# Transposes moved between halves of products, scores of two row halves interleaved, and head outputs turned by pairs, in two transformer blocks on one core

## The chip, the cores and the metric

One core of a Trainium2 chip runs the kernel in one launch. The metric is the device time in microseconds, the median of the runs. TensorE's work is named by its MATMUL rows; a transpose is a matmul against the identity and is a MATMUL row too.

## What is computed

Two transformer blocks behind one another on 256 tokens of width 1024, all in float32. Cut to what the change touches:

```python
# first block: 8 heads of differential attention (2 halves of 64), 4 retention heads
qa, ka, va, qr, kr, vr, gr, gate_a, gate_r = split(rms_norm(x, g_mix) @ w_in)
probs = softmax(qa_h_c @ ka_h_c.T * 64 ** -0.5 - slope_h * dist)      # halves c = 0, 1
ya_h = (probs[0] - lam * probs[1]) @ va_h
yr_h = (qr_h @ kr_h.T * decay_h) @ vr_h
x = x + (sigmoid(gate_a) * (norm(ya) @ w_branch_diff)
         + sigmoid(gate_r) * (silu(gr) * norm(yr) @ w_branch_ret)) @ w_out
...
# second block: gated feed-forward, then two attentions of 8 heads, then feed-forward
c_q, c_kv, k_rope, mq, mk, mv = split(rms_norm(x, mix_norm) @ w_in)
a_out = softmax(q_h @ k_h.T * 96 ** -0.5) @ v_h        # "l": q from c_q, k and v from c_kv, rope
b_out = softmax(mq_h @ mk_h.T * 64 ** -0.5 - slope_h * dist) @ mv_h   # "b"
x = x + concatenate([a_out, b_out]) @ w_out
x = x + 0.5 * swiglu(rms_norm(x, ffn2_norm), w_gate, w_up, w_down)
```

## The kernel before

**Products.** Each weight arrives in units of 128 x 2048 numbers. ScalarE rounds a unit (`hi`, w_hi), VectorE subtracts (`lo`, w_lo, written over the raw unit), and TensorE makes three matmuls of each product: high times high, high times low, low times high. Activations are split likewise: `turn` transposes blocks into a work bank, ScalarE writes the high part and VectorE the low part (`split`), and the second of them frees the bank. Rows of tokens are two blocks (tb 0 and 1).

**Work banks.** All transposes and all attention outputs use two PSUM banks, 6 and 7, in turn: `WB`, built by `work_batches`, numbers every use, an even number is one bank, an odd one the other. `work_free` makes TensorE wait until the last but one use has been read out. Scores use banks 4 and 5 in the same way (`SM`).

**Order.** Each engine has its own program, written out by hand, and strictly in that order; semaphores tie them together.

**First attention.** Loop over 16 column blocks cb of w_in. From cb 6 on a step transposes the weights of head cb-6 (`diff_turn`, L), issues the scores of the next head (`diff_scores`, two halves of 64 rows, each a 128-wide and a 256-wide matmul) and then the outputs of head cb-6 (`diff_out`, which needs ScalarE's copy aT of the turned weights). At cb 7 and 8 the q and k of the retention heads are transposed first (`("qk", cb - 1, tb)`). `ret_scores` stands at the end of cb 11 to 14. A float32 matmul of a score or an output is two MATMUL rows on the chip.

**Second attention.** Products of w_in into cq, ckv, mq, mk, mv; after mq's, the transposes of mq, cq and ckv; after mv's, those of mk. Then queries of the l heads (`queries(0)`), the first b scores, `queries(1)`. Four b pairs follow (`pair`): weights of head 2j turned, scores of head 2j+2, weights of 2j+1, scores of 2j+3, then other work beside (`keys_values`, `turn_queries`, `turn_keys`), then the outputs of the pair in one bank, normalized by VectorE into src (`pair_y`). The l pairs are the same with 96-row scores and parts of the output product beside. ScalarE copies the turned weights of even heads, VectorE those of odd heads. `exps` is ScalarE's exponential, `block_logits` VectorE's part ahead of it.

**Output product.** src holds 8 column blocks: l heads in 0 to 3, b heads in 4 to 7. `("cat", tb, 1)` turns the b part of a row block after the last b pair, `("cat", tb, 0)` the l part after the last l pair. w_out has four units of 256 rows (`O2_ROWS`), `output(n, tb)` is 12 matmuls. The sum of row block 0 is complete with `output(3, 0)`, then comes `output(2, 1)`, then the transposes of the new x (`src_turn("ffn2", 0)`), `output(3, 1)`, and the second feed-forward (`gated`).

## Time and profile before

| | |
|---|---|
| median of 3 runs | 1019.09 us (1019.06 to 1019.16) |
| the profiled execution | 1019.27 us |
| its span, first to last instruction | 1017.3 us |
| mean granted TensorE clock | 0.998 of full |
| busy: TensorE / VectorE / ScalarE / GpSimd | 995.5 / 571.9 / 504.7 / 63.9 us |
| the chain that ended last | TensorE 94%, VectorE 3%, ScalarE 1% |
| DMA | 175.63 MB, mean 173 GB/s |

Busy time of TensorE is the union of its rows, and the rows overlap, since matmuls are pipelined: a 512-wide one is shown with 390 ns and starts less than that behind the one before. So distances are read from start to start. In the timeline an idle time in brackets counts from the end of the row before; the time lost is longer, as a row's tail would have been overlapped.

### The profile page before, as it was taken

To read this page: it belongs to the slowest core of one execution; us is meant where nothing else is said; L and a number is where in the kernel's file an instruction comes from. 1 tells how busy PE (TensorE), PEld (TensorE's weight loads), DVE (VectorE), ACT (ScalarE), POOL (GpSimd) and SP (SyncE) were. 2 spreads that over 40 slices of the span, in tenths; PEclk is the share of its full clock that TensorE was granted. 3 is DMA by queue.
4 is the path that set the end of the run, shared out by engine and by line. 5 is a ranking of instruction groups with operands and counts; after the bars stand their busy time and mean duration, and the time that the engine had idled before them with its cause. 6 is when DMAs were issued, how large, how long until landed. Compare 5 with 4: busy or idle time off the path is not lost.

```text
span 1017.3 us, 12900 instructions
## 1 busy us (share of the span) xinstructions
PE 995.5 (98%) x4744; PEld 821.1 (81%) x4744; DVE 571.9 (56%) x769; ACT 504.7 (50%) x700; POOL 63.9 (6%) x94
## 2 busy tenths in 40 slices
PE   8999999999999999999989999999999999999997
PEld 5888788888888888888778888888877888888885
DVE  5645555477675455545675455547555575555443
ACT  6545555644374444445663434346557464444431
POOL 3100000020020000000220000000111000000000
PEclk9999999999999999999999999999999999999999
DMA  9755554434475454545545565545551155555531
GB/s 352 228 166 166 165 166 152 149 129 165 167 255 194 178 195 166 205 169 185 184 140 204 173 200 179 193 147 167 175 204 63 44 187 184 197 176 204 169 122 42
DMA packets 98864, 175.63 MB, mean 173 GB/s; under 512 B 5936, under 2 KB 54016, under 8 KB 98816
## 3 DMA queue, kind: packets, MB, share of 16 engines
q1 hardware_dynamic: 97312, 171.73, 48.8%
q0 software_dynamic: 1344, 3.19, 1.1%
q8 instruction: 31, 0.51, 0.2%
q14 instruction: 17, 0.14, 0.1%
q10 hardware_dynamic: 160, 0.07, 0.0%
HBM read 173.91 MB, written 1.05 MB: 172 GB/s over the span
## 4 chain that ended last, share of the span: by engine, by line
PE 94%; DVE 3%; ACT 1%; issue 1%; POOL 1%; DVEq 0%; POOLq 0%; ACTq 0%
PE bank L496 85%; PE bank L510 5%; PE bank L555 1%; PE bank L554 1%; DVE w_lo L1375 1%; ACT hA_hi L986 0%; PE bank L566 0%; POOL ms L1875 0%; PE bank L607 0%; DVE hA_lo L1388 0%; PE bank L568 0%; PE bank L567 0%; PE bank L848 0%; PE bank L847 0%; PE bank L846 0%
## 5 line engine op out<-in xcount | busy, mean ns | idle before, releaser
L1375 DVE TENSOR_TENSOR w_lo<-raw,w_hi 128x2048 fp32r<-128x2048 f32 (+1 forms) x162 | 365.6, 2262 | 218.3 <-ACT w_hi L974 218.2
L974 ACT ACTIVATE w_hi<-raw 128x2048 fp32r<-128x2048 f32 (+1 forms) x162 | 306.4, 1894 | 153.2 <-PE bank L496 152.9
L496 PE MATMUL bank<-w_hi,hA_hi 128*128 128x512 f32 (+1 forms) x880 | 342.6, 395 | 6.9 <-DVE hA_lo L1388 2.6
L496 PE MATMUL bank<-w_hi,hA_lo 128*128 128x512 f32 (+1 forms) x880 | 336.6, 388 | 0.0
L496 PE MATMUL bank<-w_lo,hA_hi 128*128 128x512 f32 (+1 forms) x880 | 336.1, 388 | 0.0
L496 PEld LDWEIGHTS bank<-w_hi,hA_hi 128*128 128x128 f32 x880 | 164.9, 188 | 41.8 <-DVE hA_lo L1388 3.0
L496 PEld LDWEIGHTS bank<-w_hi,hA_lo 128*128 128x128 f32 x880 | 165.1, 188 | 34.7
L496 PEld LDWEIGHTS bank<-w_lo,hA_hi 128*128 128x128 f32 x880 | 165.4, 188 | 32.2
L496 PE MATMUL bank<-w_hi,fT_hi 128*128 128x512 f32 x304 | 93.9, 390 | 0.0
L496 PE MATMUL bank<-w_hi,fT_lo 128*128 128x512 f32 x304 | 93.6, 389 | 0.0
L496 PE MATMUL bank<-w_lo,fT_hi 128*128 128x512 f32 x304 | 93.6, 389 | 0.0
L981 ACT ACTIVATE fT_hi<-bank 128x256 fp32r<-128x256 f32 (+1 forms) x60 | 23.4, 439 | 117.7 <-PE bank L510 117.7
L496 PEld LDWEIGHTS bank<-w_hi,fT_lo 128*128 128x128 f32 x304 | 57.1, 188 | 11.9
L496 PEld LDWEIGHTS bank<-w_lo,fT_hi 128*128 128x128 f32 x304 | 57.1, 188 | 11.9
L496 PEld LDWEIGHTS bank<-w_hi,fT_hi 128*128 128x128 f32 x304 | 56.8, 188 | 11.6
L1383 DVE TENSOR_TENSOR fT_lo<-bank,fT_hi 128x256 fp32r<-128x256 f32 (+1 forms) x60 | 27.1, 491 | 63.0 <-ACT fT_hi L981 62.8
L1875 POOL TENSOR_SCALAR ms<-ss 128x1 f32<-128x1 f32 x16 | 10.3, 645 | 632.3 <-ACT junk L1004 632.0
L1215 ACT ACTIVATE act_r<-bank,rs 128x256 f32<-128x256 f32 x44 | 20.9, 475 | 57.5 <-PE bank L496 55.0
L1388 DVE SCALAR_TENSOR_TENSOR hA_lo<-bank,g_col,hA_hi 128x128 fp32r<-128x128 f32 x96 | 26.1, 344 | 22.1 <-ACT hA_hi L986 22.0
L1033 ACT ACTIVATE L<-L,mn 128x128 f32<-128x128 f32 x64 | 28.4, 458 | 10.0 <-DVE mn L1415 10.0
L1658 DVE SCALAR_TENSOR_TENSOR act_f<-bank,rs,act_r 128x256 f32<-128x256 f32 x44 | 21.2, 481 | 21.6 <-ACT act_r L1215 21.6
L986 ACT ACTIVATE hA_hi<-bank,g_col 128x128 fp32r<-128x128 f32 x96 | 26.3, 382 | 13.7 <-PE bank L510 13.1
(250 smaller groups left out, 765.2 us busy)
## 6 DMA issues: line engine op xcount, KB each, us to landing
raw<-in_w_in SPq DMA_DIRECT2D x74, 512.0 KB, 4.5
raw<-in_w_ff SPq DMA_DIRECT2D x64, 512.0 KB, 3.9
raw<-in_ffn_w_gate SPq DMA_DIRECT2D x44, 512.0 KB, 3.6
raw<-in_ffn_w_up SPq DMA_DIRECT2D x44, 512.0 KB, 4.5
raw<-in_ffn_w_down SPq DMA_DIRECT2D x44, 512.0 KB, 4.0
raw<-in_w_out SPq DMA_DIRECT2D x16, 512.0 KB, 4.2
raw<-in_w_branch_diff SPq DMA_DIRECT2D x8, 512.0 KB, 3.7
raw<-in_w_branch_ret SPq DMA_DIRECT2D x8, 512.0 KB, 3.7
```

What stands on the lines that cost most here:

```text
L496: mm = pe.matmul(o, a, w, start=first and t == 0 and m < len(outs), stop=last and t == n - 1 and m >= len(todo) - len(outs))
L510: mm = pe.transpose(work(name)[0:cols, col:col + rows], blk, ident)
L974: act.activation(w_hi[u % HI_SLOTS][:, 0:w], raw[u % RAW_SLOTS][:, 0:w], ACT.Copy).then_inc(hi_ready, 1)
L981: act.activation(dst, b, ACT.Copy).then_inc(split_hi, 1)
L986: act.activation(dst[:, n, :], b[:, n, :], ACT.Copy, scale=g_col[:, c0 + n:c0 + n + 1]).then_inc(split_hi, 1)
L1033: e = act.activation(L[:, m % 4, c], L[:, m % 4, c], ACT.Exp, bias=mn[:, m, tb:tb + 1], scale=-1.0, accum_out=sm[:, m, tb:tb + 1])
L1215: act.activation(act_r[:, tb, 0:SUB], up(tb)[:, 0:SUB], ACT.Silu, scale=inv_rms(norm, tb))\
L1375: vec.tensor_tensor(w_lo[u % RAW_SLOTS][:, 0:w], raw[u % RAW_SLOTS][:, 0:w], w_hi[u % HI_SLOTS][:, 0:w].bitcast(f32), ALU.subtract).then_i ...
L1383: vec.tensor_tensor(dst, b, hi.bitcast(f32), ALU.subtract).then_inc(work_out[WB[name] % 2], 1)
L1388: vec.scalar_tensor_tensor(out=dst[:, n, :], in0=b[:, n, :], scalar=g_col[:, c0 + n:c0 + n + 1], in1=hi[:, n, :].bitcast(f32), op0=ALU.mul ...
L1658: vec.scalar_tensor_tensor(out=act_f[:, tb, 0:SUB], in0=up(tb)[:, SUB:2 * SUB], scalar=rs[:, n:n + 1], in1=act_r[:, tb, 0:SUB], op0=ALU.mu ...
L1875: link(pool.tensor_scalar(m, s, 1.0 / width, EPS, ALU.mult, ALU.add))
```

## The change

**First attention.** The numbers of the work banks follow the new places. At cb 7 and 8 the transposes of the retention q or k no longer stand first: row block 0's come after the scores, row block 1's after the outputs. At cb 13, where no differential scores are left, `ret_scores(2)` stands between the weights' transposes and the outputs, and no longer at the end. `half_scores` writes the two halves' 128-wide matmuls and then the two 256-wide ones.

**Second attention.** cq is transposed after the first quarter of mv's product, ckv after the second, mk after the third; the first b scores come before both query products, and ScalarE's exponentials before its query copies. In a pair both heads' weights are turned first, then both heads' scores of the next pair follow, interleaved for b. The transposes of the outputs are four uses of a work bank, one per two pairs (`("cat", n)`, both row blocks): cat 2 after b pair 2, cat 3 after the first output product, cat 0 after l pair 2, cat 1 after l pair 3. Whole output products stand beside the l pairs, and `output(2, 1)` comes before `output(3, 0)`.

```diff
@@ -99 +99 @@
-        if k in (1, 2, 3, 4, 7, 8):
+        if k in (1, 2, 3, 4):
@@ -102 +102 @@
-            order += [("a", k - 6), ("v", k - 6)]
+            order += [("a", k - 6), ("qk", k - 1, 0), ("v", k - 6), ("qk", k - 1, 1)] if k in (7, 8) else [("a", k - 6), ("v", k - 6)]
@@ -121 +121,3 @@
-    order += [("cat", tb, 1) for tb in range(TB)]
+        if j == 2:
+            order += [("cat", 2)]
+    order += [("cat", 3)]
@@ -124 +126,3 @@
-    order += [("cat", tb, 0) for tb in range(TB)]
+        if j == 2:
+            order += [("cat", 0)]
+    order += [("cat", 1)]
@@ -450,0 +455,2 @@
+        if kind == "cat":
+            return [t[:, 2 * name[1]:2 * name[1] + 2, :] for t in hA], b[:, :].rearrange("p (k t) -> p k t", t=SEQ)
@@ -556,0 +563,10 @@
+        def half_scores(names, q, k, h):
+
+            halves = [(score(name), slice(c * DHD, (c + 1) * DHD)) for c, name in enumerate(names)]
+            if SM[names[0]] >= 2:
+                pe.wait_ge(score_out, SM[names[1]] - 1)
+            for b, half in halves:
+                pe.matmul(b[:, 0:P], q[half, h, 0:P], k[half, h, 0:P], start=True, stop=True)
+            for b, half in halves:
+                pe.matmul(b[:, P:384], q[half, h, P:SEQ], k[half, h, :], start=True, stop=True).then_inc(score_done, 1)
+
@@ -558,3 +574 @@
-            for c in range(2):
-                half = slice(c * DHD, (c + 1) * DHD)
-                scores(("d", h, c), qaT[half], kaT[half], h)
+            half_scores([("d", h, c) for c in range(2)], qaT, kaT, h)
@@ -604,0 +619,3 @@
+        def qk_turn(cb, tb):
+            turn(("qk", cb - 1, tb), [qk_tm[(cb - 1) % 2][:, tb, j * P:(j + 1) * P] for j in range(4)])
+
@@ -638 +655 @@
-            if cb in (1, 2, 3, 4, 7, 8):
+            if cb in (1, 2, 3, 4):
@@ -641,2 +658 @@
-                    turn(("qk", cb - 1, tb),
-                         [qk_tm[(cb - 1) % 2][:, tb, j * P:(j + 1) * P] for j in range(4)])
+                    qk_turn(cb, tb)
@@ -656,0 +673,5 @@
+                else:
+                    ret_scores(cb - 11)
+                if cb in (7, 8):
+                    pe.wait_ge(proj_out, 2 * cb)
+                    qk_turn(cb, 0)
@@ -657,0 +679,2 @@
+                if cb in (7, 8):
+                    qk_turn(cb, 1)
@@ -664 +687 @@
-            if 11 <= cb < 15:
+            if 11 <= cb < 15 and cb != 13:
@@ -822 +845 @@
-        def head_scores(kind, h):
+        def pair_scores(kind, j):
@@ -824,2 +847 @@
-                half = slice(h % 2 * BD, h % 2 * BD + BD)
-                scores(("b", h), mqT[half], mkT[half], h // 2)
+                half_scores([("b", 2 * j), ("b", 2 * j + 1)], mqT, mkT, j)
@@ -827 +849,2 @@
-                scores(("l", h), qT, kT, h)
+                for h in (2 * j, 2 * j + 1):
+                    scores(("l", h), qT, kT, h)
@@ -835,2 +858,2 @@
-                if 2 * j + 2 < BH:
-                    head_scores(kind, h + 2)
+            if 2 * j + 2 < BH:
+                pair_scores(kind, j + 1)
@@ -850,0 +874,21 @@
+        def heads_turn(name, buf, cb):
+            pe.wait_ge(proj_out, 2 * cb + 2)
+            for tb in range(TB):
+                turn((name, tb), [buf[:, tb, b * P:(b + 1) * P] for b in range(4)])
+
+        def mq_turn():
+            heads_turn("mq", mq_tm, CB_IN2 + 2)
+
+        def cq_turn():
+            pe.wait_ge(c_src, 4)
+            for tb in range(TB):
+                turn(("cq", tb), [cq[:, tb, k * P:(k + 1) * P] for k in range(3)])
+
+        def ckv_turn():
+            turn(("ckv",), [ckv[:, tb, k * P:(k + 1) * P] for k in range(2) for tb in range(TB)])
+
+        def mk_turn():
+            heads_turn("mk", mk_tm, CB_IN2 + 3)
+
+        between = {(0, 0): cq_turn, (0, 1): ckv_turn, (1, 0): mk_turn, (1, 1): lambda: None}
+
@@ -867,6 +911,4 @@
-                    mm.then_inc(unit_used, 1)
-            if n in (3, 4):
-                name, buf = (("mq", mq_tm), ("mk", mk_tm))[n - 3]
-                pe.wait_ge(proj_out, 2 * cb)
-                for tb in range(TB):
-                    turn((name, tb), [buf[:, tb, b * P:(b + 1) * P] for b in range(4)])
+                        if tb:
+                            mm.then_inc(unit_used, 1)
+                        if n == 4:
+                            between[j, tb]()
@@ -874,4 +916 @@
-                pe.wait_ge(c_src, 4)
-                for tb in range(TB):
-                    turn(("cq", tb), [cq[:, tb, k * P:(k + 1) * P] for k in range(3)])
-                turn(("ckv",), [ckv[:, tb, k * P:(k + 1) * P] for k in range(2) for tb in range(TB)])
+                mq_turn()
@@ -918,2 +957 @@
-            if n % 2 == 0:
-                turned(("cat", tb, 1 - n // 2))
+            turned(("cat", O2_ROWS[n]))
@@ -928 +965,0 @@
-        queries(0)
@@ -931,2 +968,2 @@
-        for h in range(2):
-            head_scores("b", h)
+        pair_scores("b", 0)
+        queries(0)
@@ -934,0 +972,5 @@
+        def cat_turn(n):
+
+            turned((("l" if n < 2 else "b") + "v", 2 * (n % 2) + 1))
+            turn(("cat", n), [src[:, tb, (2 * n + k) * P:(2 * n + k + 1) * P] for k in range(2) for tb in range(TB)])
+
@@ -936,0 +979,2 @@
+            if j == 2:
+                cat_turn(2)
@@ -939,5 +983 @@
-        for h in range(2):
-            head_scores("l", h)
-        turned(("bv", BH // 2 - 1))
-        for tb in range(TB):
-            turn(("cat", tb, 1), [src[:, tb, (4 + k) * P:(5 + k) * P] for k in range(4)])
+        pair_scores("l", 0)
@@ -945,2 +985,4 @@
-        for j, beside in enumerate((lambda: output_step(0, 1), lambda: output_step(1, 0), lambda: output(1, 1, t1=1),
-                                    None)):
+        cat_turn(3)
+
+        for j, beside in enumerate((lambda: output_step(0, 1), lambda: output_step(1, 0), lambda: output_step(1, 1),
+                                    lambda: output(2, 0))):
@@ -948,6 +990,3 @@
-        turned(("lv", MH // 2 - 1))
-        for tb in range(TB):
-            turn(("cat", tb, 0), [src[:, tb, k * P:(k + 1) * P] for k in range(4)])
-        output(1, 1, t0=1).then_inc(unit_used, 1)
-        output(2, 0)
-        output(3, 0).then_inc(acc_done, 1)
+            if j == 2:
+                cat_turn(0)
+        cat_turn(1)
@@ -954,0 +994 @@
+        output(3, 0).then_inc(acc_done, 1)
@@ -1284,9 +1324,8 @@
                         act.activation(junk[:, 0:cols], buf[:, tb, 0:cols], ACT.Square, accum_out=ssc[:, k:k + 1])\
                            .then_inc(csq, 1)
-            if n == 4:
-                split(("cq", 0))
-                split(("cq", 1))
-                split(("ckv",))
             hi(U0["in2"] + 3 + 2 * n)
+        split(("cq", 0))
+        split(("cq", 1))
+        split(("ckv",))
         in2_copy(4)
         hi(U0["ukv"])
@@ -1315,8 +1354,8 @@
                                ACT.Copy).then_inc(heads_out[1], 1)
 
-        queries_copy(0)
-        hi(U0["o2"])
         for h in range(2):
             exps(SOFT["b", h], SM["b", h])
+        queries_copy(0)
+        hi(U0["o2"])
         queries_copy(1)
         hi(U0["o2"] + 1)
@@ -1332,17 +1371,18 @@
         heads_copy(0, qT)
         hi(U0["o2"] + 2)
+        split(("cat", 2))
         pair("b", 3, True)
         heads_copy(MH // 2, kT)
         hi(U0["o2"] + 3)
-        for tb in range(TB):
-            split(("cat", tb, 1))
         for h in range(2):
             exps(SOFT["l", h], SM["l", h])
+        split(("cat", 3))
         for j in range(MH // 2):
+            if j == 3:
+                split(("cat", 0))
             pair("l", j, j == MH // 2 - 1)
             if j == 1:
                 hi(U0["f2"])
-        for tb in range(TB):
-            split(("cat", tb, 0))
+        split(("cat", 1))
         hi(U0["f2"] + 1)
         squares("ffn2", 0)
@@ -1811,8 +1851,8 @@
         for tb in range(TB):
             turned_copy(("mq", tb), mqT[:, :, tb * P:(tb + 1) * P])
+        lo(U0["in2"] + 9)
         split(("cq", 0))
         split(("cq", 1))
         split(("ckv",))
-        lo(U0["in2"] + 9)
         lo(U0["uq"])
         for tb in range(TB):
@@ -1829,18 +1869,19 @@
         pair_y("b", 2)
         lo(U0["o2"])
+        split(("cat", 2))
         pair("b", 3, True)
         heads_copy(MH // 2, kT)
         pair_y("b", 3)
         next_pair("l", 0)
-        for tb in range(TB):
-            split(("cat", tb, 1))
         lo(U0["o2"] + 1)
+        split(("cat", 3))
         for j in range(MH // 2):
+            if j == 3:
+                split(("cat", 0))
             pair("l", j, j == MH // 2 - 1)
             pair_y("l", j)
             if j < 2:
                 lo(U0["o2"] + 2 + j)
-        for tb in range(TB):
-            split(("cat", tb, 0))
+        split(("cat", 1))
         lo(U0["f2"])
         lo(U0["f2"] + 1)
```

How TensorE's order moves around the last b pair. Before, from the second outputs of pair 2 to the transposes of the keys (mv: values, L: weights, src: normalized outputs, aT: turned weights):

```order
L846 MATMUL bank<-mv,aT_119 128x64 [waits work_out1]
L847 MATMUL bank<-mv,aT_119 128x64
L848 MATMUL bank<-mv,aT_119 128x64
L510 MATMUL bank<-masks,L 128x128 [waits work_out1,exp_ready]
L510 MATMUL bank<-masks,L 128x128 x2
L510 MATMUL bank<-masks,L 128x128 [waits work_out0,exp_ready]
L510 MATMUL bank<-masks,L 128x128 x2
L900 MATMUL bank<-masks,k_tm 96x128 [waits heads_out1,heads_out0,k_full]
L900 MATMUL bank<-masks,k_tm 96x128 x15
```

With the change:

```order
L869 MATMUL bank<-mv,aT_119 128x64 [waits work_out1]
L870 MATMUL bank<-mv,aT_119 128x64
L871 MATMUL bank<-mv,aT_119 128x64
L516 MATMUL bank<-masks,src 128x128 [waits work_out1]
L516 MATMUL bank<-masks,src 128x128 x3
L516 MATMUL bank<-masks,L 128x128 [waits work_out0,exp_ready]
L516 MATMUL bank<-masks,L 128x128 x2
L516 MATMUL bank<-masks,L 128x128 [waits work_out1,exp_ready]
L516 MATMUL bank<-masks,L 128x128 x2
L939 MATMUL bank<-masks,k_tm 96x128 [waits heads_out1,heads_out0,k_full]
L939 MATMUL bank<-masks,k_tm 96x128 x15
```

The transposes of src (cat 2) now stand between pair 2's outputs and pair 3's weights, and the second weights' bank (work_out1) is the one that cat 2 has used.

VectorE in the same place, before (src<-bank: pair 2's outputs, w_lo: weight subtraction, aT: pair 3's odd weights):

```order
L1766 RECIPROCAL rsm<-sm 128x4 [waits exp_ready]
L1769 TENSOR_TENSOR src<-bank,rsm 128x2x2x64 [waits work_done,vec_step]
L1375 TENSOR_TENSOR w_lo_76<-raw_70,w_hi_84 128x2048 [waits hi_ready]
L1778 COPY aT_119<-bank 128x384 [waits work_done]
L1785 COPY kT<-bank 96x512 [waits heads_done] x2
```

and with the change:

```order
L1806 RECIPROCAL rsm<-sm 128x4 [waits exp_ready]
L1809 TENSOR_TENSOR src<-bank,rsm 128x2x2x64 [waits work_done,vec_step]
L1415 TENSOR_TENSOR w_lo_76<-raw_70,w_hi_84 128x2048 [waits hi_ready]
L1423 TENSOR_TENSOR hA_lo<-bank,hA_hi 128x512 [waits split_hi]
L1818 COPY aT_119<-bank 128x384 [waits work_done]
L1825 COPY kT<-bank 96x512 [waits heads_done] x2
```

The low part of cat 2 (hA_lo) stands behind the weight subtraction.

VectorE at the end of the output products, with the change (before, the first row is two splits of 128x4x128 with the same place behind the last output, and the rest is the same):

```order
L1809 TENSOR_TENSOR src<-bank,rsm 128x2x2x64 [waits work_done,vec_step]
L1423 TENSOR_TENSOR hA_lo<-bank,hA_hi 128x512 [waits split_hi]
L1415 TENSOR_TENSOR w_lo_80<-raw_74,w_hi_84 128x2048 [waits hi_ready]
L1415 TENSOR_TENSOR w_lo_75<-raw_69,w_hi_81 128x2048 [waits hi_ready]
L1447 SCALAR_TENSOR_TENSOR x<-bank,x 128x512 [waits acc_done]
L1447 SCALAR_TENSOR_TENSOR x<-bank,x 128x512
```

TensorE ahead of the transposes of x, before (w_hi_82, w_lo_78: the unit of `output(2, 1)`):

```order
L496 MATMUL bank<-w_lo_78,hA_hi 128x512 x2
L496 MATMUL bank<-w_hi_82,hA_lo 128x512 x2
L510 MATMUL bank<-masks,x 128x128 [waits work_out0,half_sum]
L510 MATMUL bank<-masks,x 128x128 x3
L510 MATMUL bank<-masks,x 128x128 [waits work_out1,acc_out]
```

and with the change (w_hi_83, w_lo_79: the unit of `output(3, 0)`, whose end completes row block 0's sum):

```order
L502 MATMUL bank<-w_lo_79,hA_hi 128x512 x2
L502 MATMUL bank<-w_hi_83,hA_lo 128x512 x2
L516 MATMUL bank<-masks,x 128x128 [waits work_out0,half_sum]
L516 MATMUL bank<-masks,x 128x128 x3
L516 MATMUL bank<-masks,x 128x128 [waits work_out1,acc_out]
```

The last work before the transposes is now that which they depend on, through VectorE's x<-bank.

## Rows read from the trace of the kernel before

**Rows 1.** The page, busy time of TensorE (us, share of the span, instructions).
```profile
PE 995.5 (98%) x4744; PEld 821.1 (81%) x4744; DVE 571.9 (56%) x769; ACT 504.7 (50%) x700; POOL 63.9 (6%) x94
```

**Rows 2.** TensorE timeline, one diff head: start us, us, engine, line, out<-in, count.
```profile
93.40 0.50 PE L554 MATMUL bank<-kaT,qaT 64*128 64x128 f32 x4
...
94.26 0.49 PE L566 MATMUL bank<-va,aT 128*128 128x128 f32 x2
```

**Rows 3.** TensorE timeline, second attention, b pair 1.
```profile
764.79 0.33 PE L846 MATMUL bank<-mv,aT 128*128 128x64 f32 x2
...
766.07 0.50 PE L510 MATMUL bank<-masks,L 128*128 128x128 f32 x3
```

**Rows 4.** TensorE timeline, first attention behind q's transposes (idle, releaser in brackets).
```profile
107.44 0.52 PE L510 MATMUL bank<-masks,L 128*128 128x128 f32 x3 [0.44 <-DVE qrT L1495]
```

**Rows 5.** TensorE timeline, block 13 of the first attention.
```profile
189.71 0.49 PE L510 MATMUL bank<-masks,L 128*128 128x128 f32 x3
190.83 0.46 PE L566 MATMUL bank<-va,aT 128*128 128x128 f32 x2 [0.63 <-issue]
```

**Rows 6.** TensorE timeline, inputs of the second attention turned.
```profile
735.72 1.03 PE L510 MATMUL bank<-masks,mq_tm 128*128 128x128 f32 x8
737.19 1.05 PE L510 MATMUL bank<-masks,cq 128*128 128x128 f32 x6 [0.44 <-DVE mqT L1792]
738.88 0.66 PE L510 MATMUL bank<-masks,ckv 128*128 128x128 f32 x4 [0.64 <-DVE cT_lo L1383]
```

**Rows 7.** TensorE timeline, first b scores, queries, first weights turned.
```profile
754.41 0.50 PE L554 MATMUL bank<-mkT,mqT 64*128 64x128 f32 x4
...
755.27 0.45 PE L496 MATMUL bank<-w_hi,cT_hi 128*128 128x384 f32 x1
...
758.36 0.34 PE L496 MATMUL bank<-w_hi,cT_lo 128*128 128x384 f32 x1
759.30 0.52 PE L510 MATMUL bank<-masks,L 128*128 128x128 f32 x3 [0.61 <-issue]
...
761.93 0.50 PE L496 MATMUL bank<-w_hi,cT_hi 128*128 128x512 f32 x1
```

**Rows 8.** VectorE, then ScalarE timeline, first b logits and exponentials.
```profile
755.48 0.29 DVE L1415 CUSTOM_DVE_ANT_0 L<-bank,bias 128x128 f32<-128x128 f32 x1 [1.99 <-PE bank L555]
...
756.92 1.28 ACT L1033 ACT_TABLE_LOAD   x1
...
759.99 1.03 ACT L1298 ACTIVATE q_tm<-bank,rsc 128x384 f32<-128x384 f32 x2
```

**Rows 9.** TensorE timeline, b pair 2's outputs and pair 3's weights.
```profile
778.27 0.39 PE L848 MATMUL bank<-mv,aT 128*128 128x64 f32 x2
...
779.34 0.52 PE L510 MATMUL bank<-masks,L 128*128 128x128 f32 x3 [0.34 <-DVE src L1769]
```

**Rows 10.** ScalarE rounding and VectorE split in the second attention.
```profile
778.55 1.91 ACT L974 ACTIVATE w_hi<-raw 128x2048 fp32r<-128x2048 f32 x1
...
785.78 1.29 DVE L1383 TENSOR_TENSOR hA_lo<-bank,hA_hi 128x512 fp32r<-128x512 f32 x2 [0.42 <-ACT hA_hi L981]
```

**Rows 11.** TensorE timeline, first l scores and first output product.
```profile
783.10 0.49 PE L554 MATMUL bank<-kT,qT 96*128 96x128 f32 x2 [0.21 <-DVE kT L1785]
...
786.58 0.47 PE L496 MATMUL bank<-w_hi,hA_hi 128*128 128x512 f32 x1 [1.02 <-issue]
```

**Rows 12.** TensorE timeline, last l pair and last outputs turned.
```profile
806.40 0.55 PE L510 MATMUL bank<-masks,L 128*128 128x128 f32 x3 [0.18 <-ACT L L1033]
807.28 0.55 PE L510 MATMUL bank<-masks,L 128*128 128x128 f32 x3 [0.33 <-ACT L L1033]
...
809.95 1.09 PE L510 MATMUL bank<-masks,src 128*128 128x128 f32 x8 [0.59 <-DVE src L1769]
```

**Rows 13.** VectorE, then TensorE timeline, end of the output products.
```profile
812.48 4.48 DVE L1375 TENSOR_TENSOR w_lo<-raw,w_hi 128x2048 fp32r<-128x2048 f32 x2
...
820.44 1.04 PE L510 MATMUL bank<-masks,x 128*128 128x128 f32 x8
```

More of the change, by code:

```diff
@@ L1315, in heads_copy @@
                                ACT.Copy).then_inc(heads_out[1], 1)
+        for h in range(2):
+            exps(SOFT["b", h], SM["b", h])
         queries_copy(0)
         hi(U0["o2"])
-        for h in range(2):
-            exps(SOFT["b", h], SM["b", h])
         queries_copy(1)
```

2 lines of the change are left out of this document (1 added, 1 removed).

## The prediction

> **What bounds the kernel now.** I read the page first: TensorE is busy 98% of the span [rows 1], at the full granted clock. VectorE and ScalarE are busy about half of it, so a term of the sum is TensorE time: work that it no longer does, or a wait that it gains or loses. Then I read TensorE's timeline in the two attentions, start to start, because ends overlap. Transposes follow one another every 0.11 us (eight in 1.03 us with the tail [rows 6]), twelve 512-wide product matmuls take 2.86 us (761.93 to 764.79 [rows 3, 7]), the twelve small matmuls of a pair's outputs 1.28 us [rows 3]. What lies above such spacings is waiting.
>
> **Side by side, first attention: nothing.** The eight matmuls of a head's two halves start in one group and the next work starts 0.86 us after the first (93.40 to 94.26 [rows 2]). A lone 64-row score of the second attention has four matmuls and also takes about 0.85: six transposes and two such scores take 2.63 (759.30 to 761.93 [rows 7]), 0.03 of it the start after a wait. So neighbouring halves already run beside each other in the written order of before, and writing them interleaved has nothing left to win but some 0.01 us a head. I take 0.
> The Trainium skill ("TensorE: Matmul & The Clock Gate", Part 3, "What overlaps and what doesn't") says that matmuls stay in strict program order in start and end. By that rule the first half's second matmul would block the other half, the old order would show about 1.4 us a head, and the new one would win some 0.5 on each of 8 heads and the first pair. The rows show 0.86, so the trace disagrees with it; the sum goes by the row.
>
> **First attention, moved steps.** The q and k turns now stand behind the weights' turn and the scores. Before, the weights' turn waits for a bank copy, start to start 0.60 us too late at both places [rows 4], the same pattern as 737.19 behind eight transposes [rows 6]. Now qk's second half shares a bank with its first; between them lie only the outputs' 0.61 us, while copy and handover need about 1.15 from the last transpose. That leaves 0.33 to 0.43 to wait: gain 0.27 each, **-0.54**. In block 13 nothing covered the copy of the last weights: 190.83 is 0.79 late [rows 5]. Retention scores (about 0.66) now fill that, and vanish where they stood: **-0.65**.
>
> **Second attention, inputs.** Waits behind mq's eight transposes (0.60), behind cq's (1.03 over 0.11 spacing) and for the first exponentials (759.30 comes 0.94 after the last query matmul, 0.17 is normal: 0.77) [rows 6, 7]. cq, ckv and mk now stand between halves of the last product, 2.8 us apart, and copies need under 2.2. The scores go before both query products, 6.4 us (18 matmuls in 3.2 [rows 7]). All three waits go: **-2.40**.
> ScalarE gets a new queue. With S the start of the first scores: mv copy done S+0.75, weight rounding 1.9 [rows 10], table load and four exponentials 3.07 (756.92 to 759.99), query copies 0.92, rounding 1.85, copies 1.03 [rows 8]: S+9.5, handed over at S+9.6. TensorE is at the keys' product at S + 0.86 + 6.4 + 0.77 (six transposes) + 0.86 = S+8.9: **+0.70**.
>
> **Pairs of heads.** b: six transposes and two single scores, 2.60 without that 0.03, become six transposes and one doubled score, 0.76 + 0.86 = 1.62. Three times: **-2.95**. The l heads use 96 rows, not halves: no gain. But the second transposes of pairs 1 and 2 now follow the first ones at once, and their bank is the previous pair's output, released by VectorE 0.95 after its last matmul; this is the existing wait of 0.50 at 779.34 [rows 9]. Scores used to cover it. Four places: **+2.00**.
>
> **Outputs turned by pairs.** A cat turn takes the bank that the next-but-one turn needs, and ScalarE and then VectorE must split it: VectorE starts 0.63 after ScalarE, takes 0.69 (two parts in 1.29 [rows 10]), and the handover is 0.13. The largest wait is in b's last pair. Let X be the start of b6's and b7's scores. ScalarE: first logits X+1.07 (754.41 to 755.48 [rows 7, 8]), first exponential 0.67 later, exponentials 1.77 (what 3.07 leaves without the table load), two copies of qT 0.96 (as the 1.03 of [rows 8]), rounding 1.8 (778.55 [rows 10]), and only then its part of cat 2: X+6.3. VectorE's weight subtraction, 2.2 (half of 4.48 [rows 13]), ends before its turn comes. The bank is free at X+6.3+0.63+0.69+0.13 = X+7.7. TensorE: scores 0.86, sixteen transposes 1.79, outputs 1.28, cat turn 0.44, ba6 after a wait of 0.40 and 0.35: it wants the bank at X+5.1. So ba6 waits 0.4 and ba7 2.6, against 0.50 before: **+2.50**. Bounds for ba7: 0.5 (only an output's release) to 3.2 (0.6 more); I take the chain, since each link stands in program order.
> At la1 the bank is cat 3's: from its last transpose 0.31 to ScalarE and the 1.45 above, less la0's three transposes and one spacing, 0.44: **+1.33** (0.5 to 1.5). For it, kT's wait at 783.10 (0.38) and the wait for both splits at 786.58 (1.18) go [rows 11]: **-1.56**. At the last l pair the waits for exponentials and bank (0.35, 0.49, and 0.12 in front of the outputs) go [rows 12], **-0.96**, since a whole output product now stands before it; the pattern of ba6 and ba7 returns without weight operations in it: la6 0.39, la7 1.76 from the turn less 0.11, 0.39 and 0.36, so 0.90: **+1.29** (0.9 to 1.6). The 0.75 before the last cat turn at 809.95 [rows 12] stays.
>
> **The tail.** Product work is the same, but before, 42 product matmuls (9.6 us) lay between the last cat turn and the turn of x at 820.44 [rows 13], and the sum for row block 0 was complete 12 matmuls before it. Now 24 lie there, and x's turn follows the sum at once. VectorE still has two subtractions, 4.48 together, ahead of x_add [rows 13]; they start after cat 1's split, 1.5 us behind the turn, and end 0.4 after TensorE is done. Then 0.69 for the first half and a handover: about 1.0, and 0.2 for the second half: **+1.20** (0.2 if VectorE were free and x_add half as long, 1.8 if everything comes 0.6 later). Norm splits for the feed-forward follow with 0.5 us to spare: 0.
>
> **Sum.** -0.54 -0.65 -2.40 +0.70 -2.95 +2.00 +2.50 -1.56 +1.33 -0.96 +1.29 +1.20 = -0.04 us. About 9.1 us is won and 9.0 given back. The profiled execution took 1019.27 us (span 1017.3 and 1.97 around it); the median of the runs is 0.18 lower. So 1019.23 beside it, **1019.1** as a median. A measurement of this kernel tells about 0.2%, 2.0 us, from no change.
>
> **Rivals.**
> 1. *The bank waits are short* (faster). If ScalarE and VectorE reach the splits of cat 2, 3 and 0 in time, ba7, la1 and la7 cost only 0.5 each, as at 779.34: -2.1 -0.8 -0.4, 1015.8; ba7 alone gives 1017.0. For it: both engines are half idle, and a small shift of the 1.9 and 2.3 us operations ahead of the split decides. Against: these stand ahead of it in order. Chance 0.24.
> 2. *The tail runs late* (slower). x_add, squares, rounding and subtraction of the normalized rows stand in a chain behind the two subtractions. TensorE's first gated product needs them 2.8 us after x's turn. If the chain is more than 0.5 us longer than I add up, that product stalls, and so does the next multiply: VectorE has only some 0.3 us to spare there. Another 0.6 for x and 1.6 for the stall: 1021.3. With ba7 at its upper end 1021.9. Against: each link has room of its own. Chance 0.12.
> 3. *Interleaving does more than nothing*, by the order rule above: 9 groups at 0.5 us, 1014.6. Only if the group in [rows 2] is not what it seems. Chance 0.03.
>
> **How the numbers follow.** The forecast, waits replacing waits, holds 0.61; its own terms add up to about 1017.4 to 1020.8. Rivals 1 and 3 are mostly beyond 2.0 us faster, rival 2 beyond 2.0 slower; part of rival 1 (ba7 alone, partly) falls just inside. Faster 0.24, same 0.64, slower 0.12. The range for 8 in 10 reaches a little beyond ba7 alone on the one side, and to the edge of the tail case on the other: 1016.7 to 1021.0.
>
> **What would show it.** Right: score groups of a diff head still 0.86; every b pair one group of eight matmuls; the turn at 107.44 and the output at 190.83 no longer late; a TensorE gap of 2 to 3 us before the second transposes of b's last pair, released by VectorE's hA_lo; gaps near 1 us before la1, la7 and the turn of x. Wrong: no such gap (rival 1), gaps in the first feed-forward products (rival 2), or diff score groups shorter than 0.86 (rival 3). Most of all the forecast is wrong if the split of cat 2 starts before the weight operations end.

## The result, and the profile after

| | before | with the change |
|---|---|---|
| median of 22 runs each | 1019.08 us (1018.82 to 1020.60) | 1020.56 us (1018.92 to 1025.30) |
| ratio, 95% interval | | 1.0021 (1.0013 to 1.0029) |
| the profiled execution, its span | 1019.27, 1017.3 us | 1023.88, 1021.9 us |
| its mean granted clock | 0.998 | 0.993 |
| busy: TensorE / VectorE / ScalarE | 995.5 / 571.9 / 504.7 us | 998.2 / 573.2 / 504.7 us |

The change costs 1.5 us where none was forecast, and the runs now spread over 6.4 us. They fall into groups, and time goes with the mean granted clock: 1018.92 twice (0.999), thirteen at 1019.92 to 1020.60 (0.996 to 0.997), two at 1021.1 to 1021.3 (0.994), and five at 1023.88 to 1025.30 (0.991 to 0.993). TensorE has 2.7 us more busy time for the same 4744 instructions [rows 1]. So some of them ran slower.

**The clock.** A table by stretches of 2 us of the changed kernel's profile (the busy us and number of instructions of each engine, then TensorE's granted clock):

```profile
core 0: us, PE busy (x) PEld busy (x) DVE busy (x) ACT busy (x) POOL busy (x), PEclk, DMA share, GB/s
...
774.00:776.00 2.00, 0.53 (x4) 0.31 (x3) 2.00 (x2) 2.00 (x3) 0.00 (x0) 1.00 0.00 0
776.00:778.00 2.00, 0.80 (x8) 0.83 (x9) 1.24 (x3) 0.70 (x2) 0.00 (x0) 1.00 0.00 0
778.00:780.00 2.00, 2.00 (x15) 1.95 (x14) 1.55 (x4) 0.59 (x1) 0.00 (x0) 0.65 0.03 8
780.00:782.00 2.00, 2.00 (x12) 2.00 (x11) 0.13 (x2) 1.79 (x2) 0.00 (x0) 0.50 0.00 0
...
786.00:788.00 2.00, 2.00 (x6) 1.60 (x5) 2.00 (x1) 0.99 (x4) 0.00 (x0) 0.50 0.00 0
788.00:790.00 2.00, 2.00 (x10) 1.60 (x9) 0.18 (x1) 0.00 (x0) 0.00 (x0) 0.79 0.00 0
```

At 774 to 778 TensorE is busy 1.33 us of 4. Then the clock goes from 1.00 to 0.50 (1.2 GHz in place of 2.4) and comes back in the stretch from 788. From the granted clock of these stretches (1.40 us of half clock up to 780, all of the 8 us to 788, 0.84 us behind it) the slow stretch is 10.24 us long, 778.55 to 788.79. At half speed that costs 5.1 us, and 1023.88 less 5.1 is 1018.8, the group at full clock. TensorE's timeline there (start, us, and in brackets the idle time ahead and its releaser), which answers to [rows 9]:

```profile
774.25 0.52 PE L516 MATMUL bank<-masks,L 128*128 128x128 f32 x3 [0.23 <-DVE src L1809]
777.20 0.52 PE L516 MATMUL bank<-masks,L 128*128 128x128 f32 x3 [2.43 <-DVE hA_lo L1423]
777.55 2.62 PE L939 MATMUL bank<-masks,k_tm 128*96 128x128 f32 x16
779.97 0.53 PE L869 MATMUL bank<-mv,aT 128*128 128x64 f32 x2
```

The second weights' transposes of b's last pair come 2.95 us after the first ones, which need 0.36: a wait of 2.59 where the prediction has 2.6, for the releaser it names. The sixteen transposes of the keys behind it start 0.11 us apart at first and 0.21 at the end: 2.42 us to the next start instead of 1.75. ScalarE and then VectorE in front of that wait, in the order that the prediction's chain follows:

```profile
773.00 1.05 ACT L1353 ACTIVATE qT<-bank 96x512 f32<-96x512 f32 x2
773.95 1.90 ACT L1014 ACTIVATE w_hi<-raw 128x2048 fp32r<-128x2048 f32 x1
775.75 0.57 ACT L1021 ACTIVATE hA_hi<-bank 128x512 fp32r<-128x512 f32 x1
```

```profile
774.02 2.28 DVE L1415 TENSOR_TENSOR w_lo<-raw,w_hi 128x2048 fp32r<-128x2048 f32 x1
776.36 0.69 DVE L1423 TENSOR_TENSOR hA_lo<-bank,hA_hi 128x512 fp32r<-128x512 f32 x1
```

**The first attention**, TensorE's timeline at a common head, at cb 7 and at cb 13, answering to [rows 2, 4, 5]:

```profile
93.42 0.49 PE L569 MATMUL bank<-kaT,qaT 64*128 64x128 f32 x4
93.75 0.60 PE L571 MATMUL bank<-kaT,qaT 64*128 64x256 f32 x4
94.28 0.49 PE L580 MATMUL bank<-va,aT 128*128 128x128 f32 x2
```

```profile
108.19 0.39 PE L582 MATMUL bank<-va,aT 128*128 128x128 f32 x2
108.69 0.55 PE L516 MATMUL bank<-masks,qk_tm 128*128 128x128 f32 x3
```

```profile
189.73 0.38 PE L602 MATMUL bank<-qrT,krT 128*128 128x128 f32 x2
190.09 0.46 PE L580 MATMUL bank<-va,aT 128*128 128x128 f32 x2
```

The eight score matmuls take 0.86 us, as before. The outputs' last matmul at 108.19 and the next transposes are 0.50 apart instead of 0.22: a wait of 0.28 (0.33 to 0.43 forecast). At 190.09 only 0.13 is left of 0.79.

**The second attention**: first scores of pair 1 and first keys and values; then the second transposes of l's first and last pair, the last turn of the heads and that of x, answering to [rows 7, 11 to 13]:

```profile
756.24 0.49 PE L569 MATMUL bank<-mkT,mqT 64*128 64x128 f32 x4
756.56 0.60 PE L571 MATMUL bank<-mkT,mqT 64*128 64x256 f32 x4
757.78 0.73 PE L502 MATMUL bank<-w_hi,cT_hi 128*128 128x512 f32 x2 [0.62 <-ACT q_tm L1337]
```

```profile
791.68 0.52 PE L516 MATMUL bank<-masks,L 128*128 128x128 f32 x3 [1.18 <-DVE hA_lo L1423]
...
812.56 0.52 PE L516 MATMUL bank<-masks,L 128*128 128x128 f32 x3 [0.75 <-DVE hA_lo L1423]
...
817.70 0.66 PE L516 MATMUL bank<-masks,src 128*128 128x128 f32 x4 [0.59 <-DVE src L1809]
...
824.77 1.25 PE L516 MATMUL bank<-masks,x 128*128 128x128 f32 x8 [0.93 <-DVE x L1447]
```

The waits are where the prediction has them and about as long. Start to start, less the normal spacing: 0.69 at the first keys and values (0.70 forecast), 1.34 at la1 (1.33), 0.91 at la7 (0.90), 1.09 at the turn of x (1.0). The eight transposes of x take 1.01 us to the next start, 0.22 more than before (0.2 forecast).

### The profile page after: what moved, and what is told of

Read it like the earlier page. It is cut to its first block, busy times and chain, and to the rows that moved or that the text cites. A ratio compares the mean times of both kernels' runs of the same rounds, so it can differ in the third digit from the quotient of the medians.

```text
span 1021.9 us, 12906 instructions
## 1 busy us (share of the span) xinstructions
PE 998.2 (98%) x4744; PEld 823.5 (81%) x4744; DVE 573.2 (56%) x769; ACT 504.7 (49%) x700; POOL 66.0 (6%) x94
## 4 chain that ended last, share of the span: by engine, by line
PE 92%; DVE 3%; ACT 3%; issue 1%; POOL 1%; DMA 0%; DVEq 0%; POOLq 0%; SPq 0%; ACTq 0%
PE bank L502 84%; PE bank L516 5%; DVE w_lo L1415 1%; ACT w_hi L1014 1%; ACT hA_hi L1026 0%; PE bank L571 0%; PE bank L561 0%; PE bank L569 0%; DMA raw<-in_w_in 0%; PE bank L580 0%; ACT L L1073 0%; PE bank L871 0%; PE bank L870 0%; POOL ms L1916 0%; PE bank L869 0%
```

## The experiments

Three theories. **A**: the clock falls because TensorE does so little around the wait of 2.59 us, and that is all the forecast missed. **B**: it falls for something else in this stretch, or by the executions and not by the kernel. **C**: the missing time is in waits elsewhere. All medians stand beside the kernel before on the same chip (median of its runs in the table). The changed kernel has its 1020.56 beside a kernel before of 1019.08, 0.04 to 0.24 us lower than those in the table, so a difference from it is uncertain by that much.

| run | median us (lowest to highest) | before | ratio, 95% interval |
|---|---|---|---|
| fill | 1018.90 (1018.19 to 1018.95) | 1019.32 | 0.9995 (0.9986 to 1.0004) |
| swap | 1017.63 (1016.94 to 1017.77) | 1019.32 | 0.9982 (0.9973 to 0.9991) |
| before_wait | 1020.09 (1019.56 to 1021.77) | 1019.32 | 1.0010 (1.0001 to 1.0019) |
| first_only | 1017.88 (1017.17 to 1017.99) | 1019.32 | 0.9984 (0.9975 to 0.9993) |
| halves_only | 1018.96 (1018.73 to 1020.76) | 1019.12 | 0.9998 (0.9989 to 1.0007) |
| no_cat | 1014.69 (1014.14 to 1016.45) | 1019.12 | 0.9955 (0.9942 to 0.9969) |
| before_wait_fill | 1019.91 (1019.83 to 1021.48) | 1019.12 | 1.0015 (1.0006 to 1.0024) |
| rearranged | 1012.63 (1012.46 to 1012.75) | 1019.12 | 0.9937 (0.9924 to 0.9951) |
| turn_late | 1016.43 (1016.02 to 1016.50) | 1019.23 | 0.9972 (0.9960 to 0.9983) |
| inputs_only | 1016.72 (1016.11 to 1018.40) | 1019.23 | 0.9979 (0.9970 to 0.9988) |
| before_wait_fill2 | 1020.33 (1020.03 to 1020.45) | 1019.23 | 1.0010 (1.0001 to 1.0019) |
| rearranged2 | 1010.63 (1010.01 to 1010.90) | 1019.23 | 0.9914 (0.9900 to 0.9927) |

### fill: the wait stays, TensorE works in it

```diff
                 pe.wait_ge(exp_ready, m + 1)
+                if (kind, h) == ("b", 7):
+                    warm_up(10)
                 turn((kind + "a", h), ...)
```

> The changed kernel, with ten spare bf16 matmuls (128x512, of a buffer of zeros) put on TensorE between the wait for the last block head's exponentials and that head's weights turn, where the profile shows a wait of 2.59 us. They write a score bank that nobody reads before the next scores overwrite it. The wait stays as long; only what TensorE does in it changes. Theory A (TensorE's granted clock falls to half because it does so little around that wait, and that is all that the forecast missed): the clock stays at 1.00 through 778 to 790 us, the median is 1018.9 to 1019.1 instead of 1020.56, and the spread of 6.4 us over the runs shrinks to that of the kernel before. Rival B (the clock falls for another reason in this stretch, such as the many short transposes and half-row matmuls, or the halved clock is a matter of the executions and not of the kernel): about 1020.5 again with the same spread. Rival C (the missing 1.5 us are waits elsewhere): about 1020.5, clock 1.00.

`warm_up(10)` issues ten matmuls whose result nobody reads (the trace has records of nine). 1018.90, and 11 runs within 0.8 us, as theory A has it. The timeline of TensorE and the table by stretches:

```profile
774.13 2.11 PE L624 MATMUL bank<-junk 128*128 128x512 bf16 x9
776.42 0.55 PE L516 MATMUL bank<-masks,L 128*128 128x128 f32 x3 [0.18 <-DVE hA_lo L1425]
776.80 1.91 PE L941 MATMUL bank<-masks,k_tm 128*96 128x128 f32 x16
```

```profile
774.00:776.00 2.00, 1.95 (x10) 0.80 (x9) 1.94 (x2) 2.00 (x3) 0.00 (x0) 1.00 0.00 0
776.00:778.00 2.00, 1.82 (x16) 1.58 (x15) 1.36 (x3) 0.14 (x2) 0.00 (x0) 1.00 0.03 8
778.00:780.00 2.00, 2.00 (x20) 2.00 (x19) 0.93 (x3) 1.72 (x3) 0.00 (x0) 1.00 0.00 0
```

The second transposes still come as late behind the first. Only the spare matmuls were added, and the clock stays at 1.00. C falls, and so does B in its form "by the executions".

### swap: the wait made shorter

```diff
-        hi(U0["o2"] + 2)
         split(("cat", 2))
+        hi(U0["o2"] + 2)
```

and the same on VectorE with `lo(U0["o2"])`.

> The changed kernel, with the splitting of the third turned block of heads put ahead of a whole unit's copy on ScalarE (1.90 us) and ahead of a whole unit's low part on VectorE (2.28 us), where it stood behind both. The wait of 2.59 us on TensorE before the last block head's weights turn should shrink to about 0.7, and a wait of about 0.7 should appear at that pair's outputs, since VectorE's copy of the weights now stands behind the low part: 1.0 us less in all. Theory A (the granted clock falls from the long wait): 1017.9 to 1018.1, clock kept, a spread under 1 us. Rival B (the clock falls for another reason in this stretch): 1019.5, with several us of spread left. Rival C (only the sum of waits counts, and the clock's cost is unrelated): 1019.5 with a full clock.

The wait is 0.91 instead of 2.59, and the clock is full:

```profile
775.49 0.52 PE L516 MATMUL bank<-masks,L 128*128 128x128 f32 x3 [0.75 <-DVE hA_lo L1423]
...
779.25 0.49 PE L560 MATMUL bank<-kT,qT 96*128 96x128 f32 x2 [0.21 <-DVE kT L1825]
```

The median is 0.3 under the forecast: the wait of 0.7 that I expected at the pair's outputs did not come, since VectorE's copy was done in time. A shorter one of 0.38 came behind them, at the first l scores. From the first weights' transposes to the second l scores (774.22 to 780.01) TensorE needs 5.79 us and in fill 6.99: 1.20 less, and the medians differ by 1.27. So nothing but the waits tells these two runs apart.

### before_wait: the wait alone, in the kernel before

```diff
-        pair_y("b", 2)
         lo(U0["o2"])
+        pair_y("b", 2)
```

> The kernel before, with one unit's low part (2.28 us on VectorE) moved ahead of the third pair's block outputs. That puts a wait of about the same length, 2.6 to 2.8 us instead of 0.5, at the same weights turn as in the changed kernel, and nothing else of the change. Theory A: the clock falls to half in some executions behind that wait here too, 1021.3 at the least and up to 1027, a spread of some us. Rival C (a wait costs its length and no more): 1019.08 + 2.2 = 1021.3, spread of 0.3 us as before. Rival B (it takes the rest of the change, the head-pair turns or the side-by-side halves): also 1021.3 with no spread.

The length was misjudged: VectorE starts the low part before the outputs are there (777.47 to 779.66, the outputs' matmuls end at about 778.4), so the wait is 1.72 us and not 2.7. Eleven runs split in two: seven at 1019.56 to 1020.11, four at 1021.47 to 1021.77. The profiled one is of the upper group. TensorE's timeline and the table:

```profile
780.44 0.52 PE L510 MATMUL bank<-masks,L 128*128 128x128 f32 x3 [1.56 <-DVE src L1769]
780.79 3.41 PE L900 MATMUL bank<-masks,k_tm 128*96 128x128 f32 x16
```

```profile
778.00:780.00 2.00, 0.88 (x8) 0.64 (x7) 1.97 (x3) 2.00 (x3) 0.00 (x0) 1.00 0.03 9
780.00:782.00 2.00, 1.56 (x10) 1.55 (x11) 1.17 (x3) 0.70 (x2) 0.00 (x0) 0.75 0.03 8
782.00:784.00 2.00, 2.00 (x12) 1.91 (x10) 0.98 (x3) 0.59 (x1) 0.00 (x0) 0.50 0.00 0
```

The sixteen transposes that take 1.91 us above take 3.41 here. So nothing else of the change is needed: a wait at this place can halve the clock in the kernel before too. Here the slow stretch is about 3.4 us, and the two groups lie 1.6 apart. Only this one execution has a trace; whether the other three of the upper group fell at the same place is not shown.

### first_only and halves_only: the first attention

first_only is the kernel before with the diff's lines on `diff_scores`, `qk_turn` and `ret_scores`; halves_only has only `half_scores` in `diff_scores`.

> The kernel before with the change's first-attention part alone: the differential heads' scores side by side by row halves, the turns of the last two query and key column blocks between the halves of a head's work, and the first retention scores moved ahead. The forecast's terms for it are 0 for the interleave, -0.54 for the turns and -0.65 for the retention scores: 1019.08 - 1.19 = 1017.9. If the interleave brings something by itself, less; if the moved turns only shift a wait, 1018.5 to 1019.1.

> The kernel before with the differential heads' scores written side by side by row halves, and nothing else of the change. The forecast gave this nothing: a group of eight score matmuls takes 0.86 us in either order, since in the kernel before, too, matmuls of different row halves run beside each other. Forecast: 1019.1 to 1019.3, as before. Rival (the interleave pays, 7 groups times 0.25 to 0.4 us): 1016.5 to 1017.5. If it is neither, the run of the first-attention part alone, which measured 1.44 us less than before where 1.19 was forecast, says where the rest is from: 0.2 us less here would close that.

-1.44 and -0.16 us. Interleaving is worth nothing that can be told, as the prediction's row said. The moved steps bring a little more than the 1.19 forecast; TensorE's busy time between 100 and 200 us rises by 1.27, from 98.44 to 99.71. One run of halves_only took 1020.76, and it was the profiled one:

```profile
806.00:808.00 2.00, 1.48 (x11) 1.02 (x10) 0.67 (x2) 1.49 (x7) 0.00 (x0) 1.00 0.00 0
808.00:810.00 2.00, 1.41 (x12) 1.25 (x12) 0.82 (x3) 0.00 (x0) 0.00 (x0) 0.97 0.00 0
810.00:812.00 2.00, 2.00 (x9) 1.91 (x9) 0.40 (x1) 0.78 (x2) 0.00 (x0) 0.50 0.00 0
812.00:814.00 2.00, 2.00 (x7) 1.57 (x6) 1.84 (x3) 0.45 (x2) 0.00 (x0) 0.67 0.00 0
```

The clock falls here behind the waits of 0.35, 0.49 and 0.75 us of [rows 12]. The order there is that of the kernel before, whose own runs have five such values in 99 (1020.30 to 1020.60 at a mean clock of 0.996, against a median of 1019.1 to 1019.3): a loss of this kind was there already, but rare. No trace of those five shows its place.

### no_cat: the change without the turns by pairs

The `cat` batches, `output` and their splits are as in the kernel before, everything else is as changed.

> The changed kernel, with the head outputs turned as in the kernel before (all blocks of one branch in two batches by row block, behind its last pair, with the products, splits and tail as before); all the rest of the change stays. The forecast's terms for what stays are -0.54, -0.65, -2.40, +0.70, -2.95 and +2.00 for the bank waits at the second weights turn of four pairs: -3.84 us, 1015.2 to 1015.5. If the clock is lost through the wait that the turns by pairs of heads bring, it is full here: a spread under 1 us. If the clock is lost through the shortened scores or the bank waits, the spread of several us stays and the median is above 1016.

1014.69 (forecast 1015.2): -4.4 us. Without the turns by pairs the change is a clear gain, and four of its five runs keep the clock; the fifth (1016.45) lost it at 805 to 809 us, behind the same last waits.

### before_wait_fill and before_wait_fill2

Both are before_wait with spare matmuls added:

```diff
+                if (kind, h) in (("b", 7), ("l", 7)):
+                    warm_up(6 if kind == "b" else 2)
...
+        warm_up(3)
         turned(("lv", MH // 2 - 1))
```

The first run has `warm_up(6)` at b's last pair only, the second all three.

> The kernel before with the low part moved ahead of the third pair's block outputs (the run that fell into two groups, 1019.6 to 1020.1 and 1021.5 to 1021.8), and six spare bf16 matmuls of 128x512 (0.21 us each) put into the wait of 1.72 us that this makes. Theory A (the clock falls because TensorE does so little around the wait): the upper group is gone, all runs 1019.6 to 1020.3, clock 1.00 behind the wait. Rival: the two groups stay, since they come from something else.

Against expectation five of 11 runs were at 1021.40 to 1021.48, so filling this wait alone made the upper group no smaller than before_wait's four. The profile, of a run in that group, has the clock at 1.00 behind the filled wait, and the fall behind the last l pair:

```profile
780.00:782.00 2.00, 1.83 (x17) 1.76 (x17) 1.33 (x3) 0.91 (x3) 0.00 (x0) 1.00 0.04 8
...
810.00:812.00 2.00, 1.55 (x7) 1.55 (x8) 0.40 (x1) 0.40 (x1) 0.00 (x0) 0.62 0.00 0
812.00:814.00 2.00, 2.00 (x7) 1.63 (x7) 1.60 (x3) 0.80 (x2) 0.00 (x0) 0.53 0.00 0
```

That gave the next run its expectation:

> The run before_wait_fill again (the kernel before, the low part moved, six spare matmuls in the wait that this makes), with two more spare matmuls before the last weights turn of the last pair (wait of 0.49 us there) and three in front of the last turns of the heads (wait of 0.75 us). In that run 5 of 11 executions were 1.5 us longer, and in its profile the clock fell behind these two waits, not behind the filled one. Theory A (the clock falls because TensorE does little around waits, wherever they stand): no execution in the upper group, all 1019.8 to 1020.1, clock 1.00 from 800 to 820 us; the fills may cost up to 0.3 us where they reach beyond their wait. Rival (the upper group is a matter of the executions, or of the filled place): 3 to 7 of 11 executions at 1021.4 again.

All 11 runs at 1020.03 to 1020.45: the upper group is gone, though the runs lie up to 0.35 above the forecast. Where the spare matmuls stand:

```profile
808.04 0.60 PE L607 MATMUL bank<-junk 128*128 128x512 bf16 x2 [0.33 <-ACT L L1036]
...
810.34 0.81 PE L607 MATMUL bank<-junk 128*128 128x512 bf16 x3
```

They cost 0.3 to 0.4 us themselves, being longer than their waits, and take away 1.5 us of loss in half the runs.

### turn_late: one batch moved

```diff
-        order += [("ba", 2 * j), ("ba", 2 * j + 1), ("bv", j)]
-        if j == 2:
-            order += [("cat", 2)]
+        order += [("ba", 2 * j), ("ba", 2 * j + 1)] + [("cat", 2)] * (j == 3) + [("bv", j)]
```

with `cat_turn(2)` behind `turn_keys()` on TensorE, and both splits behind `heads_copy`.

> The changed kernel with one thing moved: the third turned block of heads (with its splitting on ScalarE and VectorE) comes behind the last keys' turns and in front of the last block pair's outputs, instead of in front of that pair's weights turns. The bank that the second weights turn waits for is then freed by the pair outputs' reader again, as in the kernel before (0.50 us), and the four transposes stand where TensorE waits for VectorE's copy of the weights. Theory A: 2.1 to 2.5 us of waits go and the clock stays full: 1018.9 - 2.3 = 1016.4 to 1016.9, spread under 1 us. If the clock's loss had another source: 1018 with several us of spread. If the first output step then waits for the split: up to 1017.6.

1016.43, spread 0.5. The timeline, against the rows of the change above:

```profile
774.02 0.52 PE L514 MATMUL bank<-masks,L 128*128 128x128 f32 x3 [0.34 <-DVE src L1809]
774.37 1.91 PE L937 MATMUL bank<-masks,k_tm 128*96 128x128 f32 x16
776.13 0.63 PE L514 MATMUL bank<-masks,src 128*128 128x128 f32 x4
776.60 0.43 PE L867 MATMUL bank<-mv,aT 128*128 128x64 f32 x2
```

The bank wait is 0.50 again, and the transposes of the heads fill the time until VectorE's copy is there. One batch in another place is worth 4.1 us of median: 2.5 of waiting and 1.6 of clock.

### inputs_only

The lines of the diff on `between`, `mq_turn` and the order of queries, exponentials and splits, in the kernel before.

> The kernel before with the second attention's input turns put between the halves of the last projections, and the first block scores ahead of the first queries, and nothing else of the change. The forecast's terms: -2.40 for the inputs and +0.70 for the new wait at the first keys and values, 1019.1 - 1.7 = 1017.4. The run without the head-pair turns measured 0.6 us less than the sum of its terms, of which 0.2 is known to be from the first attention: if the rest is from here, 1017.0.

1016.72, -2.5: the -2.40 is right, but the +0.70 is not in it. With single scores in the pairs the keys' product starts late enough for ScalarE's copies. The 0.69 appears only with the doubled scores, so it belongs to their term. Three of 11 runs lost 1.6 us (mean clock 0.996).

### rearranged and rearranged2: the gains without the waits

rearranged: cat turns beside work; a pair's scores and other work between its two weights turns; ScalarE's second query copy ahead of weight roundings; half steps of the output product where TensorE waited at the end.

```diff
             for h in (2 * j, 2 * j + 1):
                 ...
-            if 2 * j + 2 < BH:
-                pair_scores(kind, j + 1)
+                if h == 2 * j:
+                    if h + 2 < BH:
+                        pair_scores(kind, j + 1)
+                    if middle:
+                        middle()
```

> An attempt to keep the change's gains and drop its waits. The head-pair blocks are turned beside work and in front of the pair's outputs, so that no weights turn waits for their splitting; a pair's scores, the first half of the last keys' turns and half an output step stand between its two weights turns, which covers the four bank waits of 0.50 us and the waits of 2.59, 1.34 and 0.91; ScalarE copies the second queries ahead of two units' high parts (wait of 0.70 at the first keys and values); at the end, half steps of the output product stand where TensorE waited 0.75 and 1.09. The waits listed sum to 10.1 us in the run with spare matmuls, of which the clock's theory leaves nothing extra. If two thirds to nine tenths of them go: 1009.8 to 1012.2. If VectorE or ScalarE is the bound behind them and the waits only move: 1013 to 1016. With the clock full, the spread stays under 1 us.

> The rearranged kernel with the waits that its profile still shows taken on: the first half of the keys' turns waits only for its own banks, with a query copy ahead of one head's exponentials on ScalarE (wait of 0.94 us); the splits of two head blocks stand ahead of the next pair's exponentials and logits (0.66); the second sum of the output comes ahead of a unit's low part (0.81); the squares of the last norm come behind its splits (0.81); and two low parts move into VectorE's idle stretches beside the keys and values. Sum 3.2 us: 1012.63 - 3.2 = 1009.4 if all go, 1009.4 to 1011 forecast; 1012 and more if the moved low parts or copies make new waits.

1012.63 and 1010.63 us: the first is just above its forecast (1009.8 to 1012.2), the second within its own. The second is 8.6 us faster than before (0.9914) and 9.9 below the change. Some waits moved instead of going. In rearranged2 the keys' turn starts at once, but the cat turn behind it now waits for a copy of ScalarE that stands behind a weight rounding:

```profile
772.95 1.04 PE L937 MATMUL bank<-masks,k_tm 128*96 128x128 f32 x8
774.87 0.63 PE L511 MATMUL bank<-masks,src 128*128 128x128 f32 x4 [0.88 <-ACT aT L1094]
```

All runs of both are within 0.9 us.

## Why the prediction was wrong

**The step that failed** is in its first paragraph, "a term of the sum is TensorE time: work that it no longer does, or a wait that it gains or loses". I read 0.998 as a full clock and took it as a constant. The term +2.50 therefore prices the wait of ba7 by its length. The runs show a second price: 20 of 22 runs lose clock, 1.0 to 6.4 us each, 1.6 in the median. The profiled one loses it behind that wait, and fill, which puts work into that wait and changes nothing else, has no such run in 11 and lands at 1018.90. In before_wait a wait of 1.72 us at the same place brings the loss into the kernel before. No rival had it either. The measured 1020.56 lies inside the forecast range, but by luck: the range reached that far for a late tail, which did not come.

The Trainium skill ("TensorE: Matmul & The Clock Gate", Part 1, "What's actually happening") says that the array's clock is halved or full by how busy the engine has been of late. It also says that the number of slow matmuls at the start of one and the same kernel differs from run to run. The prediction cites the page for another rule and does not weigh this one. By it a loss of clock stood against the change wherever a long wait was added; the trace agrees with the two levels (0.50 and 1.00), and the run times fall into four groups, though the loss here is in the middle of the kernel and not at its start.

**Point by point.**
- Side by side, 0: right (0.86 in both orders; halves_only -0.16, within its interval). Rival 3 is out.
- Moved steps of the first attention, -1.19: -1.44 measured, busy time says -1.27; the new waits are 0.28, not 0.33 to 0.43.
- Inputs, -2.40: -2.5 measured. +0.70: right in size (0.69), though it comes with the pairs.
- Pairs, -2.95 and +2.00: each b pair is one group of eight of 0.86 us, and the four bank waits are 0.50 each. Together with the first two points -3.84; no_cat gives -4.4. Of the missing 0.6, 0.1 to 0.25 is in the first attention; the rest I have not placed.
- Turns by pairs: 0.39 and 2.59 at b's last pair, 1.34, 0.39, 0.91 at the l pairs, as forecast to 0.01 us.
- Tail, +1.20: 1.09 at the turn of x and 0.22 within it, and no stall in the feed-forward behind it. Rival 2 is out.
- The sum, -0.04: the two runs at full clock are 0.16 below the median of before, and fill is 0.42 below on its chip. As a sum of waits and work it holds, in part by two errors that offset one another: no_cat is 0.6 under its terms, and fill is 4.0 above no_cat where the terms for the turns by pairs and the tail make 3.8. As a forecast of the time it lacked one term.
- Rival 1 asked the right question, how late the split comes, and swap and turn_late show what it is worth (1.3 and 2.5 us against the runs at full clock). Its condition did not hold.

**Still open**: why the slow stretch is 10.24 us in the profile of the change and about 3.4 in the others. Only one execution of each kernel has a trace, so that the thirteen runs 1.0 to 1.7 us above the fastest have a stretch of the short kind is an estimate from the cost in before_wait. And which waits bring a fall: those of 1.59 and 1.73 us at 502 and 517 us, between 512-wide products, never did in fourteen profiles, while waits of about 0.50 and 0.75 whose ends lie 2.6 to 2.7 us apart (0.35 ahead of them in two cases), among small matmuls, did in three and did not in others with the same rows, the kernel before among them.

## What to carry to other kernels

Price a new wait twice: by its length, and, among small matmuls, by what it can do to TensorE's clock; a table of busy time and clock by stretches of 2 us shows the places. If the runs of a kernel spread into groups, compare their mean clocks before looking for a cause elsewhere. A small split that frees a bank should not stand in queue order behind a whole unit's 1.9 or 2.3 us; where it must, let other work of TensorE, useful or spare, fill the time.

## What the hardware showed that I had not expected

- Ten spare bf16 matmuls whose result nobody reads make the changed kernel 1.7 us faster in the median (fill), and five more make the runs of before_wait_fill even.
- Waits of 0.35, 0.49 and 0.75 us near each other can halve the clock for some 3.4 us (halves_only, before_wait_fill). Runs that are longer by such a loss are one in 20 with the order of before, and five of 11 in before_wait_fill, where all of that stands 0.6 us later. Whether the shift in time is what makes the difference is not shown; before_wait has it too, so that its upper group may be partly from there.
- In the profile of the change the clock falls 1.35 us after the long wait has ended (777.20), at 778.55, when TensorE is at full work again: the first slow instructions are not those beside the gap. In before_wait the fall comes about 0.5 us after the wait, in halves_only less than 0.1.
